# Two transformer blocks in one fp32 kernel: the first block's inverse roots multiplied into the accumulators, GpSimd's low parts in pieces, and two smaller moves

## The chip, the cores and the metric

One core of one Trainium2 chip. The metric is the device time of one execution in microseconds (us). PE is TensorE, ACT ScalarE, DVE VectorE, POOL GpSimd, SP SyncE, which issues most DMAs.

## What is computed

A residual stream x of 512 tokens by 1024 runs through two blocks of two layers each, all in float32. Block 1, in each layer:

```python
h = rms_norm(x, attn_norm_g[l])                 # x * rsqrt(mean(x*x) + eps) * g
rq, rk, rv, rg, dq, dk, dv = split(h @ w_in[l])
ret = rms_norm(retention_bidir(rq, rk, rv, ...), ret_norm_g[l]) * silu(rg)
da = rms_norm(diff_attention(norm(dq), norm(dk), dv, lam, slopes), diff_norm_g[l]) * (1 - lam_init)
x = x + concat([ret, da]) @ w_out[l]
h = rms_norm(x, ffn_norm_g[l])
x = x + (silu(h @ w_gate[l]) * (h @ w_up[l])) @ w_down[l]
```

Block 2 carries 256 context tokens beside the 512 in its first layer (768 columns), has neighbourhood attention in layer 0 and sliding-window attention (swa) in layer 1, a gated FFN with a depthwise convolution, and a modulation: `mod = silu(c) @ w_mod + b_mod` gives shifts, scales and gates, 96 rows of w_mod tiles in all, computed by DVE while block 1 runs.

## The kernel before

Everything is transposed: features on the 128 partitions, tokens (S = 512, or T2 = 768) along the free axis. xT holds the stream in 8 tiles. **A unit** is one 128-column slice of a weight matrix times all of h: K tiles (8, or 11 in the down projections), three matmuls each, since float32 is made from two fp32r parts (hi*hi + hi*lo + lo*hi). 364 units run in the order that schedule() lists. They go in pairs (par 0 and 1) over two sets of w_raw, w_hi and w_lo and two PSUM accumulators acc[0], acc[1].

The weights' chain of a unit: SP loads w_raw (weights, L500); once PE is done with the unit before the last, ACT casts it to w_hi (hi_part, L1178; each stage calls it as split(par) after mm_done); POOL writes w_lo = w_raw - w_hi in one instruction (L556); PE waits for w_lo_ready (unit, from L647). SP waits with the next w_raw until w_lo is ready. In the FFN's down projection the first pair interleaves its two units (LATE_LAST), since its last input tile comes late.

**Norms.** In the residual stage before a norm, DVE adds the accumulator to xT (L1808), ACT squares the tile (L1236), DVE sums six of the squares (L1815). PE packs the sums into one bank (L820), ACT takes the root (L1252), DVE inverts it (L1669), PE spreads it over the tokens (L827), and then, tile by tile: DVE multiplies x, gain and inverse root (n_xn, L1683), ACT makes h_hi (L1259), DVE or POOL h_lo (L1701, L612). The next pair of units (fresh_pair, L701) follows tile by tile. norm() runs so for all eight norms; at the start of the program it squares and packs each tile as it lands.

**After a unit.** In block 1's projections ACT copies the accumulator to proj1 (take_out, L1301; Silu for rg), and for dq, dk DVE does (head_norm, L1732), with a norm per head behind it: squares on ACT, sums (head_sums) and spreads (head_casts) on PE between the next units' matmuls, as `tail` for the last pair. In the gated FFN (glu, L1342 and L1825) unit par 0 is the gate, par 1 the up projection: ACT writes glu_g = Silu(acc[0]), DVE glu_a = acc[1] * glu_g (L1832), ACT b_hi, DVE b_lo (L1834). Silu, Sqrt and Exp need a table in ACT, loaded by an ACT_TABLE_LOAD where another one is in; Copy, in front of them in the first loop of an FFN, gets one too.

**Modulation** (L1626): per pair of units of block 1 two multiply-and-sum instructions on 128x1024 (L1634, L1637) and a copy of two columns (L1640), on DVE, from mod_w, which SP loads once the last pair's are done (mod_step). It stands in front of the takes in head_norm, resid and glu; beside projections DVE has nothing else.

ahead() moves the first pair's weights of a stage ahead of the norm or attention in front of it, on SP and POOL. In the swa stage SP waits for n_xn_ready (all of the norm) and loads cosine, sine and band before it loads q's weights.

## Time and profile before

| | us |
|---|---|
| median of 3 runs | 3073.2 (3066.57 to 3074.27) |
| the profiled execution | 3069.21 |
| its span, first to last instruction | 3067.4 |
| PE busy | 2981.4 (97%) |
| DVE busy | 1585.0 (52%) |
| ACT busy | 1144.6 (37%) |
| POOL busy | 1053.2 (34%) |

The mean granted clock of PE was 0.989 of full speed. A window row gives each engine's busy time in a stretch; a timeline row an instruction's start and length; behind an arrow stands what released it.

### The profile page before, as it was taken

To read this page: it belongs to the slowest core of one execution; us is meant where nothing else is said; L and a number is where in the kernel's file an instruction comes from. 1 tells how busy PE (TensorE), PEld (TensorE's weight loads), DVE (VectorE), ACT (ScalarE), POOL (GpSimd) and SP (SyncE) were. 2 spreads that over 40 slices of the span, in tenths; PEclk is the share of its full clock that TensorE was granted. 3 is DMA by queue.
4 is the path that set the end of the run, shared out by engine and by line. 5 is a ranking of instruction groups with operands and counts; after the bars stand their busy time and mean duration, and the time that the engine had idled before them with its cause. 6 is when DMAs were issued, how large, how long until landed. Compare 5 with 4: busy or idle time off the path is not lost.

```text
span 3067.4 us, 46468 instructions
## 1 busy us (share of the span) xinstructions
PE 2981.4 (97%) x16904; PEld 2398.4 (78%) x16904; DVE 1585.0 (52%) x2527; ACT 1144.6 (37%) x1735; POOL 1053.2 (34%) x458
## 2 busy tenths in 40 slices
PE   8999999999999999999999999999999899999999
PEld 6866788887857788877886687888888777878887
DVE  5357654556357544554315746541553348566372
ACT  4264441223274442232226733321332227543232
POOL 3433444443433444442220023332223240244443
PEclk9999999999999999999999999999999899999999
DMA  4421343433411344431111111121111110122222
GB/s 165 142 102 38 127 151 124 147 132 104 164 60 56 125 146 131 146 124 49 48 65 42 53 42 55 62 69 56 67 64 66 56 62 8 38 86 95 91 97 101
DMA packets 78029, 272.75 MB, mean 89 GB/s; under 512 B 8160, under 2 KB 15328, under 8 KB 77792
## 3 DMA queue, kind: packets, MB, share of 16 engines
q1 hardware_dynamic: 76256, 267.09, 26.2%
q10 hardware_dynamic: 1664, 4.18, 0.4%
q8 instruction: 72, 1.18, 0.2%
q14 instruction: 37, 0.30, 0.0%
HBM read 269.14 MB, written 2.10 MB: 88 GB/s over the span
## 4 chain that ended last, share of the span: by engine, by line
PE 58%; issue 26%; POOL 8%; DVE 5%; ACT 2%; POOLq 0%; DMA 0%; ACTq 0%; DVEq 0%
PE ps L663 43%; POOL w_lo L556 7%; PE ps L701 4%; PE ps L1085 1%; PE ps L772 1%; PE ps L1067 1%; PE ps L814 1%; DVE s_s L2081 1%; PE ps L928 1%; PE ps L917 1%; DVE s_s L2071 1%; PE ps L952 1%; PE ps L909 1%; DVE h_lo L1701 1%; PE ps L827 1%
## 5 line engine op out<-in xcount | busy, mean ns | idle before, releaser
L556 POOL TENSOR_TENSOR w_lo<-w_raw,w_hi 128x1024 fp32r<-128x1024 f32 (+1 forms) x364 | 945.0, 2596 | 1533.6 <-ACT w_hi L1178 1533.6
L663 PE MATMUL ps<-h_hi,w_hi 128*128 128x512 f32 (+1 forms) x2816 | 953.2, 372 | 8.2 <-POOL w_lo L556 4.2
L663 PE MATMUL ps<-h_hi,w_lo 128*128 128x512 f32 (+1 forms) x2816 | 945.1, 369 | 0.0
L663 PE MATMUL ps<-h_lo,w_hi 128*128 128x512 f32 (+1 forms) x2816 | 944.1, 368 | 0.0
L1178 ACT ACTIVATE w_hi<-w_raw 128x1024 fp32r<-128x1024 f32 (+1 forms) x364 | 406.4, 1116 | 1352.0 <-PE ps L663 1229.4
L663 PEld LDWEIGHTS ps<-h_hi,w_hi 128*128 128x128 f32 x2816 | 489.4, 188 | 116.2 <-issue 12.9
L663 PEld LDWEIGHTS ps<-h_hi,w_lo 128*128 128x128 f32 x2816 | 489.1, 188 | 90.8
L663 PEld LDWEIGHTS ps<-h_lo,w_hi 128*128 128x128 f32 x2816 | 488.4, 188 | 89.4 <-issue 0.7
L1855 DVE TENSOR_SCALAR conv_y<-u_pad,small 128x770 f32<-128x770 f32 (+1 forms) x88 | 176.3, 2004 | 192.2 <-ACT u_pad L1371 192.0
L1808 DVE SCALAR_TENSOR_TENSOR xT<-ps,mod,xT 128x512 f32 (+1 forms) x72 | 45.4, 659 | 306.7 <-PE ps L663 259.9
L1634 DVE CUSTOM_DVE_ANT_0 mod_junk<-mod_w,silu_c 128x1024 f32<-128x1024 f32 x96 | 139.3, 1451 | 123.5 <-DMA mod_w<-w_mod_dram 121.6
L1858 DVE SCALAR_TENSOR_TENSOR conv_y<-u_pad,small,conv_y 128x770 f32<-128x770 f32 (+1 forms) x176 | 156.1, 887 | 24.4 <-DVE conv_y L1855 6.7
L1637 DVE CUSTOM_DVE_ANT_0 mod_junk<-mod_w,silu_c 128x1024 f32<-128x1024 f32 x96 | 159.0, 1656 | 3.3
L1832 DVE TENSOR_TENSOR glu_a<-ps,glu_g 128x512 f32<-128x512 f32 x44 | 30.4, 692 | 188.7 <-PE ps L663 182.0
L1834 DVE TENSOR_TENSOR b_lo<-glu_a,b_hi 128x512 f32 x44 | 105.4, 2396 | 41.6 <-ACT b_hi L1352 41.6
L663 PE MATMUL ps<-a_hi,w_hi 128*128 128x512 f32 (+1 forms) x396 | 119.9, 357 | 1.5 <-POOL w_lo L556 1.5
L663 PE MATMUL ps<-a_lo,w_hi 128*128 128x512 f32 (+1 forms) x396 | 120.0, 357 | 0.0
L663 PE MATMUL ps<-a_hi,w_lo 128*128 128x512 f32 (+1 forms) x396 | 120.0, 357 | 0.0
L663 PE MATMUL ps<-b_hi,w_hi 128*128 128x512 f32 x264 | 104.8, 397 | 2.8 <-POOL w_lo L556 2.8
L663 PE MATMUL ps<-b_hi,w_lo 128*128 128x512 f32 x264 | 104.4, 396 | 0.0
L663 PE MATMUL ps<-b_lo,w_hi 128*128 128x512 f32 x264 | 104.4, 395 | 0.0
L1808 DVE SCALAR_TENSOR_TENSOR xT<-ps,xT 128x512 f32 (+1 forms) x48 | 33.2, 691 | 130.4 <-PE ps L663 104.4
(213 smaller groups left out, 3708.4 us busy)
## 6 DMA issues: line engine op xcount, KB each, us to landing
mod_w<-w_mod_dram SPq DMA_DIRECT2D x96, 512.0 KB, 3.5
w_raw<-w_gu_dram SPq DMA_DIRECT2D x88, 512.0 KB, 3.4
w_raw<-w_down_dram SPq DMA_DIRECT2D x64, 704.0 KB, 4.1
w_raw<-w_up_dram SPq DMA_DIRECT2D x88, 512.0 KB, 3.4
w_raw<-w_in_dram SPq DMA_DIRECT2D x56, 512.0 KB, 3.5
w_raw<-na_qkv_dram SPq DMA_DIRECT2D x24, 512.0 KB, 3.4
w_raw<-w_out_dram SPq DMA_DIRECT2D x16, 512.0 KB, 3.5
n_bias<-rpb_dram SPq DMA_DIRECT2D x24, 256.0 KB, 3.1
```

Source lines behind the costliest of these rows:

```text
L556: pool.tensor_tensor(w_lo[par][:, 0:cols], w_raw[par][:, 0:cols], w_hi[par][:, 0:cols].bitcast(F32), ALU.subtract).then_inc(w_lo_ready, 1)
L663: last = pe.matmul(acc[par][:, to:to + n], w[par][:, k * P:k * P + P], r[:, k, frm:frm + n], start=begin, stop=end)
L701: last = pe.matmul(acc[par][:, to:to + n], w[par][:, k * P:k * P + P], r[:, k, frm:frm + n], start=begin, stop=end)
L772: last[hd] = pe.matmul(bank(4 + 2 * (s % 2) + hd)[:, to:to + 2 * P], proj[half, j, queries], proj[half, 8 + j, keys], start=True, stop=True)
L814: pe.matmul(ps[:, 2048 + to:2048 + to + w], mats[half, SPREAD64 + g % 2, :], hn_rs[half, frm:frm + w], start=True, stop=True).then_inc(hn_ ...
L1178: act.activation(w_hi[par][:, 0:K * P], w_raw[par][:, 0:K * P], ACT.Copy).then_inc(w_hi_ready, 1)
L1634: dve.tensor_tensor_reduce(mod_junk[:], mod_w[:], silu_c[:, 0, :], 1.0, 0.0, ALU.mult, ALU.add, mod_sum[:, 0:1]).then_inc(mod_step, 1)
L1637: dve.tensor_tensor_reduce(mod_junk[:], mod_w[:], silu_c[:, 1, :], 1.0, 0.0, ALU.mult, ALU.add, mod_sum[:, 1:2]).then_inc(mod_step, 1)
L1808: last = dve.scalar_tensor_tensor(out=x_, in0=row(acc[par][:, to:to + n]), scalar=gate, in1=x_, op0=ALU.mult, op1=ALU.add)
L1834: dve.tensor_tensor(b_lo[:, bass.ds(f, 1), :], row(glu_a[:]), b_hi[:, bass.ds(f, 1), :].bitcast(F32), ALU.subtract).then_inc(a_lo_ready, 1)
L1855: dve.tensor_scalar(y, u, tap(0), tap(3), ALU.mult, ALU.add).then_inc(conv_step, 1)
L1858: dve.scalar_tensor_tensor(out=y, in0=u, scalar=tap(j), in1=y, op0=ALU.mult, op1=ALU.add).then_inc(conv_step, 1)
```

## The change

Seven edits, listed as what the code does:

1. Block 1's four norms become kind "late". ACT makes h_hi = xT * gain directly (hi_late), DVE h_lo from the same product; the inverse root, spread over the tokens, is kept in SBUF (rb) and multiplied in where the accumulators are taken. PE packs and spreads between the matmuls of the first pair, which runs unit 0 whole and then unit 1 (packs after step 3, spreads after step 10; at the start after 9 and 13). POOL does none of the low tiles.
2. So DVE, not ACT, takes block 1's projections (take_proj), with modulation between the two takes; rg's Silu then runs in place on ACT. In glu DVE writes glu_g = acc[0] * rb, then runs modulation, ACT takes Silu in place, DVE multiplies by rb again, then by acc[1].
3. At the start the gains are loaded first, by SP; w_raw is loaded without a wait for x's third part; the constants come last; ACT makes h_hi as x lands and squares afterwards.
4. POOL's w_lo is written by 4 instructions of a quarter each, its h_lo tiles by one per 256 columns.
5. The gated FFN's first round stands ahead of the loop in ACT's program (peel=1); a Silu on one element stands ahead of rg's.
6. In the swa stage SP loads q's first two pairs of weights before it waits for the norm and loads cosine, sine and band.
7. The casts of the swa keys' last pair come at step 10 of the next pair instead of 5.

```diff
-POOL_TILES = {"norm": (2, 4, 6), "mix": (0, 2, 5, 3, 6), "fin2": (0, 2, 4, 6)}
+POOL_TILES = {"late": (), "norm": (2, 4, 6), "mix": (0, 2, 5, 3, 6), "fin2": (0, 2, 4, 6)}
...
+        add("late" if block == 1 else "norm", block=block, layer=layer, which=which, T=T)
...
+                    weights(dict(ph, pairs=(0, 2)))
+                    sp.wait_ge(n_xn_ready, KT * (ph["norm0"] - 2 * DEPTH))
                     sp.dma_start(s_cos[:], d["rope"][0]).then_inc(tab["rope"], 16)
                     sp.dma_start(s_sin[:], d["rope"][1]).then_inc(tab["rope"], 16)
                     sp.dma_start(s_band[:], d["band"]).then_inc(tab["swa"], 16)
                 if "weight" in ph:
-                    weights(ph)
+                    weights(dict(ph, pairs=(2, 4)) if roped(ph) else ph)
...
-                        pool.tensor_tensor(w_lo[par][:, 0:cols], w_raw[par][:, 0:cols],
-                                           w_hi[par][:, 0:cols].bitcast(F32), ALU.subtract).then_inc(w_lo_ready, 1)
+                        for frm in range(0, cols, cols // PIECES):
+                            piece = slice(frm, frm + cols // PIECES)
+                            last = pool.tensor_tensor(w_lo[par][:, piece], w_raw[par][:, piece],
+                                                      w_hi[par][:, piece].bitcast(F32), ALU.subtract)
+                        last.then_inc(w_lo_ready, 1)
...
+                order = LATE_LAST if hidden else alternate(KT if late else 6 if ph["T"] == S else 3)
+                for step, (par, k) in enumerate(order):
...
+                    if late and step == (9 if first else 3):
+                        pack_norm(ph["fresh"])
+                    if late and step == (13 if first else 10):
+                        spread_norm(ph["fresh"])
...
-                    if k == 5:
+                    if k == (KT + 2 if ph["T"] == T2 and n == 2 else 5):
...
+            def hi_late(ph, k):
+
+                gain = col("g_" + ph["which"], KT * ph["layer"] + k)
+                act.activation(h_hi[:, k, 0:S], xT[:, k, 0:S], ACT.Copy, scale=gain).then_inc(h_hi_ready, 1)
+
+            def root(ph):
+                act.wait_ge(n_sum, ph["chunk0"] + len(chunks(ph["T"])))
+                act.activation(n_rs[:], n_packed, ACT.Sqrt, bias=eps1[:]).then_inc(n_std, 1)
+
+            def late_end(ph, split):
+
+                n0 = ph["norm0"]
+                hi_late(ph, 0)
+                act.wait_ge(acc_free, ph["unit0"])
+                act.wait_ge(n_added, (KT - 1) * (n0 + 1))
+                act.activation(n_sq[1][:, 0:S], xT[:, KT - 1, 0:S], ACT.Square).then_inc(n_sq_ready, 1)
+                hi_late(ph, 1)
+                hi_late(ph, 2)
+                split(1)
+                for k in range(3, KT):
+                    hi_late(ph, k)
+                root(ph)
...
+            def beginning(ph):
+
+                act.wait_ge(gains_in, 16)
+                for q in range(4):
+                    act.wait_ge(x_in[q], 16)
+                    hi_late(ph, 2 * q)
+                    hi_late(ph, 2 * q + 1)
+                    if q in (0, 2):
+                        hi_part(q // 2, 16, KT)
+                act.dma_start(lam_vec[:], d["lam"]).then_inc(loaded, 16)
+                act.dma_start(silu_c[:], d["c"]).then_inc(loaded, 16)
+                act.activation(stats[:, 20:21], eps1[:], ACT.Sqrt).then_inc(table_in, 1)
+                for k in range(KT):
+                    if k >= 2:
+                        act.wait_ge(n_added, k)
+                    act.activation(n_sq[k % 2][:, 0:S], xT[:, k, 0:S], ACT.Square).then_inc(n_sq_ready, 1)
+                root(ph)
...
+                        if ph["weight"] == "w_in":
+                            split(par)
+                            if ph["func"] == "silu":
+                                gate = dst[:, bass.ds(i * 2 + (ph["tile0"] + par), 1), 0:S]
+                                act.wait_ge(acc_free, i * 2 + (ph["unit0"] + par + 1))
+                                act.activation(gate, gate, ACT.Silu)
+                            continue
...
-                    act.activation(glu_g[:], acc[0][:, 0:S], ACT.Silu).then_inc(acc_free, 1)
+                    act.wait_ge(acc_free, f * 2 + (ph["unit0"] + 1))
+                    act.activation(glu_g[:], glu_g[:], ACT.Silu).then_inc(glu_silu, 1)
...
-                units_of(ph, body)
+                units_of(ph, body, peel=1)
...
+            def late(ph):
+
+                n0 = ph["norm0"]
+                if n0 == 0:
+                    dve.wait_ge(gains_in, 16)
+                    dve.memset(n_sum_sq[:, 0:S], 0.0).then_inc(n_added, 1)
+
+                def lo(k):
+                    dve.wait_ge(h_hi_ready, KT * ph["h0"] + k + 1)
+                    dve.scalar_tensor_tensor(out=h_lo[:, k, 0:S], in0=xT[:, k, 0:S],
+                                             scalar=col("g_" + ph["which"], KT * ph["layer"] + k),
+                                             in1=h_hi[:, k, 0:S].bitcast(F32), op0=ALU.mult, op1=ALU.subtract
+                                             ).then_inc(h_dve, 1)
+
+                def invert():
+                    dve.wait_ge(n_std, n0 + 1)
+                    dve.reciprocal(n_rs[:], n_rs[:]).then_inc(n_recip, 1)
+
+                for k in range(KT):
+                    lo(k)
+                    if k == 5 and n0:
+                        invert()
+                if n0 == 0:
+                    for k in range(KT - 2):
+                        dve.wait_ge(n_sq_ready, k + 1)
+                        dve.wait_ge(n_added, k + 1)
+                        dve.tensor_tensor(n_sum_sq[:, 0:S], n_sum_sq[:, 0:S], n_sq[k % 2][:, 0:S], ALU.add
+                                          ).then_inc(n_added, 1)
+                    invert()
+                dve.wait_ge(n_cast, ph["chunk0"] + len(chunks(S)))
+                dve.tensor_copy(halves(row(rb[:])), spread_out(S)).then_inc(n_rb, 1)
+
+            def inverted(ph):
+
+                dve.wait_ge(n_rb, ph["norm0"])
+
+            def take_proj(ph):
+
+                inverted(ph)
+
+                def take(i, par):
+                    dve.wait_ge(mm_done, i * 2 + (ph["unit0"] + par + 1))
+                    dve.tensor_tensor(proj1[:, bass.ds(i * 2 + (ph["tile0"] + par), 1), :], row(acc[par][:, 0:S]), row(rb[:]),
+                                      ALU.mult).then_inc(acc_free, 1)
+
+                with dve.Fori(0, ph["units"] // 2) as i:
+                    take(i, 0)
+                    modulation(i, ph["unit0"])
+                    take(i, 1)
...
+                inverted(ph)
                 with dve.Fori(0, FH) as f:
+                    dve.wait_ge(mm_done, f * 2 + (ph["unit0"] + 1))
+                    dve.wait_ge(a_lo_ready, BEGUN + f + n0)
+                    dve.tensor_tensor(glu_g[:], acc[0][:, 0:S], rb[:], ALU.mult).then_inc(acc_free, 1)
                     modulation(f, ph["unit0"])
-                    dve.wait_ge(acc_free, f * 2 + (ph["unit0"] + 1))
+                    dve.wait_ge(glu_silu, f + (n0 + 1))
+                    dve.tensor_tensor(glu_g[:], glu_g[:], rb[:], ALU.mult).then_inc(glu_scaled, 1)
                     dve.wait_ge(mm_done, f * 2 + (ph["unit0"] + 2))
-                    dve.wait_ge(a_lo_ready, BEGUN + f + n0)
+                    dve.wait_ge(glu_scaled, f + (n0 + 1))
                     dve.tensor_tensor(glu_a[:], acc[1][:, 0:S], glu_g[:], ALU.mult).then_inc(acc_free, 1)
```

## Rows read from the trace of the kernel before

**Rows 1.** The page, busy us (share of the span) and instructions of TensorE.
```profile
PE 2981.4 (97%) x16904; PEld 2398.4 (78%) x16904; DVE 1585.0 (52%) x2527; ACT 1144.6 (37%) x1735; POOL 1053.2 (34%) x458
```

**Rows 2.** Waits of PE: us in total, times, longest us.
```profile
PE ps L827 <- DVE n_rs L1669: 9.8, 8, 1.8
...
PE ps L663 <- POOL w_lo L556: 8.5, 9, 3.6
...
PE ps L701 <- ACT h_hi L1259: 6.5, 4, 1.6
```

**Rows 3.** Windows: stretch and its us, busy of each engine, PEclk, DMA share, GB/s.
```profile
322.70:343.10 20.40, 15.71 (x113) 11.14 (x112) 12.91 (x21) 11.44 (x16) 8.59 (x5) 0.92 0.21 70
697.30:718.00 20.70, 16.28 (x112) 12.08 (x113) 15.47 (x21) 8.35 (x13) 8.60 (x5) 0.84 0.16 51
1003.80:1024.40 20.60, 16.21 (x113) 11.87 (x112) 12.88 (x21) 11.40 (x16) 8.60 (x5) 0.83 0.21 73
17.00:35.20 18.20, 14.64 (x48) 10.41 (x48) 15.99 (x31) 10.10 (x13) 8.18 (x5) 1.00 0.31 103
2439.00:2461.80 22.80, 17.21 (x83) 12.32 (x82) 6.97 (x6) 5.85 (x7) 7.08 (x3) 0.85 0.17 56
```

**Rows 4.** Timeline, 322.5 to 328.9: start, us, engine, line, operation [idle before].
```profile
322.63 0.43 PE L820 MATMUL ps<-n_sum_sq,mats 128*32 128x64 f32 x16
...
327.92 1.29 ACT L1259 ACTIVATE h_hi<-n_xn 128x512 fp32r<-128x512 f32 x2 [2.60 <-DVE n_xn L1683]
...
328.69 0.76 PE L701 MATMUL ps<-h_hi,w_hi 128*128 128x512 f32 x1 [1.63 <-ACT h_hi L1259]
```

**Rows 5.** Timeline around two weight units, at 564 and at 465.
```profile
564.12 1.06 ACT L1178 ACTIVATE w_hi<-w_raw 128x1024 fp32r<-128x1024 f32 x1 [3.91 <-PE ps L663]
...
565.26 2.39 POOL L556 TENSOR_TENSOR w_lo<-w_raw,w_hi 128x1024 fp32r<-128x1024 f32 x1 [3.13 <-ACT w_hi L1178]
...
569.28 0.39 PE L663 MATMUL ps<-h_hi,w_hi 128*128 128x512 f32 x1
...
465.23 3.21 POOL L556 TENSOR_TENSOR w_lo<-w_raw,w_hi 128x1408 fp32r<-128x1408 f32 x1 [8.05 <-ACT w_hi L1178]
...
468.57 0.49 PE L663 MATMUL ps<-b_hi,w_hi 128*128 128x512 f32 x1 [0.72 <-POOL w_lo L556]
```

**Rows 6.** Timeline of DVE and POOL, at 469 and at 1776.
```profile
468.73 1.23 DVE L1634 CUSTOM_DVE_ANT_0 mod_junk<-mod_w,silu_c 128x1024 f32<-128x1024 f32 x1
...
469.34 3.69 POOL L556 TENSOR_TENSOR w_lo<-w_raw,w_hi 128x1408 fp32r<-128x1408 f32 x1 [0.91 <-ACT w_hi L1178]
...
469.99 4.12 DVE L1637 CUSTOM_DVE_ANT_0 mod_junk<-mod_w,silu_c 128x1024 f32<-128x1024 f32 x1
...
1776.16 0.96 DVE L1979 TENSOR_TENSOR h_lo<-proj,h_hi 128x768 fp32r<-128x768 f32 x1 [0.46 <-ACT h_hi L1471]
...
1776.95 4.39 POOL L612 TENSOR_TENSOR h_lo<-proj,h_hi 128x768 fp32r<-128x768 f32 x2 [74.76 <-ACT h_hi L1471]
...
1777.64 4.52 DVE L1979 TENSOR_TENSOR h_lo<-proj,h_hi 128x768 fp32r<-128x768 f32 x2 [0.51 <-ACT h_hi L1471]
```

**Rows 7.** Groups by line and form: count, busy us, mean ns, idle before.
```profile
L556 POOL TENSOR_TENSOR w_lo<-w_raw,w_hi 128x1024 fp32r<-128x1024 f32 x300 | 728.4, 2428 | 1218.1 <-ACT w_hi L1178 1218.1
...
L612 POOL TENSOR_TENSOR h_lo<-n_xn,h_hi 128x768 fp32r<-128x768 f32 x9 | 16.6, 1843 | 42.7 <-ACT h_hi L1259 42.7
...
L572 POOL TENSOR_TENSOR x_mask<-x_mask,r_mid 128x128 f32<-128x128 f32 x8 | 3.7, 457 | 7.5 <-ACT x_mask L1276 7.5
...
L1863 DVE TENSOR_TENSOR a_lo<-conv_z,a_hi 128x512 f32 x20 | 13.7, 686 | 0.0
...
L1178 ACT ACT_TABLE_LOAD x20 | 25.7, 1283 | 75.7 <-PE ps L663 71.8 <-PE ps L701 3.9
```

**Rows 8.** Timeline of POOL and DVE in the last conv FFN.
```profile
2744.47 2.39 POOL L556 TENSOR_TENSOR w_lo<-w_raw,w_hi 128x1024 fp32r<-128x1024 f32 x1 [2.96 <-ACT w_hi L1178]
...
2745.15 2.00 DVE L1855 TENSOR_SCALAR conv_y<-u_pad,small 128x512 f32<-128x512 f32 x1 [0.96 <-ACT u_pad L1371]
```

More of the change, by code:

```diff
@@ L124, in norm @@
     def norm(block, layer, which, T):
-        add("norm", block=block, layer=layer, which=which, T=T)
+        add("late" if block == 1 else "norm", block=block, layer=layer, which=which, T=T)
         count["norm"] += 1
@@ L186, in schedule @@
         after["fresh"] = ph if "weight" in after and ph["kind"] in POOL_TILES else None
-        ph["norm_T"] = after["T"] if after["kind"] == "norm" else None
+        ph["norm_T"] = after["T"] if after["kind"] in ("late", "norm") else None
     return phases
@@ L228 @@
 EARLY = 3
+PIECES = 4
 FRESH_ORDER = [0, 1, 2, 4, 5, 3, 6, 7]
@@ L611, in lo_tiles @@
                     pool.wait_ge(h_hi_ready, 8 * ph["h0"] + k + 1)
-                    pool.tensor_tensor(h_lo[:, k, 0:T], source(k), h_hi[:, k, 0:T].bitcast(F32), ALU.subtract
-                                       ).then_inc(h_pool, 1)
+                    for frm in range(0, T, 2 * P):
+                        last = pool.tensor_tensor(h_lo[:, k, frm:frm + 2 * P], source(k)[:, frm:frm + 2 * P],
+                                                  h_hi[:, k, frm:frm + 2 * P].bitcast(F32), ALU.subtract)
+                    last.then_inc(h_pool, 1)
             for ph in ahead(phases):
@@ L681, in fresh_pair @@
                 u0, K = ph["unit0"], ph["K"]
-                hidden = K == FH
+                hidden, late = K == FH, ph["fresh"] and ph["fresh"]["kind"] == "late"
                 hi, lo = (h_hi, h_lo) if not hidden else (b_hi, b_lo) if u0 < MOD_UNITS else (a_hi, a_lo)
                 segs = segments(ph["T"], CTX_AT if hidden else S)
-                for par, k in LATE_LAST if hidden else alternate(6 if ph["T"] == S else 3):
+                order = LATE_LAST if hidden else alternate(KT if late else 6 if ph["T"] == S else 3)
+                for step, (par, k) in enumerate(order):
                     if k == 0:
@@ L853, in normed_units @@
                     unit(ph, 0, 0, first, ends[0])
-                    unit(ph, 0, 1, first)
+                    unit(ph, 0, 1, first, ends[0])
                 def pair(i):
@@ L1148, in _ @@
                 if kind == "norm":
-                    norm(ph)
+                    pack_norm(ph)
+                    spread_norm(ph)
                 elif kind == "normed":
@@ L1226, in resid @@
                     act.wait_ge(table_in, n0 + 2)
+                late = T is not None and ph["unit0"] < MOD_UNITS and ph["unit0"] + KT < MOD_UNITS
                 def body(i, split):
@@ L1230, in body @@
                         act.wait_ge(mm_done, i * 2 + (ph["unit0"] + par + 1))
+                        if late and isinstance(i, int) and i * 2 + par == KT - 1:
+                            late_end(phases[phases.index(ph) + 1], split)
+                            continue
                         split(par)
@@ L1287, in body @@
                 def body(i, split):
+                    if ph["func"] == "silu" and i == 0:
+                        act.activation(stats[:, 23:24], eps1[:], ACT.Silu)
                     for par in range(2):
                         act.wait_ge(mm_done, i * 2 + (ph["unit0"] + par + 1))
-                        dst = proj1 if ph["T"] == S and ph["weight"] == "w_in" else proj
+                        dst = proj1 if ph["weight"] == "w_in" else proj
+                        if ph["weight"] == "w_in":
[4 more added lines that the diff above has]
+                                act.activation(gate, gate, ACT.Silu)
+                            continue
                         if ph["weight"] == "na_qkv" and i == 3 and par == 0:
@@ L1302, in body @@
                                        row(acc[par][:, 0:ph["T"]]),
-                                       ACT.Silu if ph["func"] == "silu" else ACT.Copy).then_inc(acc_free, 1)
+                                       ACT.Copy).then_inc(acc_free, 1)
                         if ph["weight"] == "swa_qkv" and par == 0:
@@ L1561, in _ @@
                     norm(ph)
-                    if ph["norm0"] == 0:
-                        condition()
+                elif kind == "late" and ph["norm0"] == 0:
+                    beginning(ph)
+                    condition()
                 elif kind == "normed":
@@ L1679, in normed @@
                     for to, _, w, c in segments(T):
-                        gain = col("g_" + ph["which"], KT * ph["layer"] + k) if ph["block"] == 1 else \
-                            gs[:, ph["layer"], w_i, k, c:c + 1]
+                        gain = gs[:, ph["layer"], w_i, k, c:c + 1]
                         if T == S:
@@ L1689, in normed @@
                                 in1=sums[0][:, to:to + w], op0=ALU.mult, op1=ALU.mult)
-                    if ph["block"] == 2 and k in POOL_TILES["norm"]:
+                    if k in POOL_TILES["norm"]:
                         last.then_inc(n_scaled, 1)
@@ L1763, in head_norm @@
                 take(0, 1)
+                if beside and h0 == 0:
+                    modulation(0, ph["unit0"])
                 if roped(ph):
@@ L2103, in _ @@
                     norm(ph)
+                elif kind == "late":
+                    late(ph)
                     if ph["norm0"] == 0:
@@ L2109, in _ @@
                         decays()
+                elif kind == "proj" and ph["weight"] == "w_in":
+                    take_proj(ph)
                 elif kind == "proj":
```

79 lines of the change are left out of this document (35 added, 44 removed).

## The prediction

> **What bounds the kernel now.** The page's busy table comes first: TensorE (PE) has a matmul running for 97% of the span [rows 1], so a gain can only come from its few idle stretches, and a loss from any new one. The waits of PE say where it idles: behind the reciprocal of the norm's root, behind the first high part of a normed tile, and behind POOL's low part of the weights [rows 2]. The windows show what a norm costs. From the last matmul of the residual stage to the first matmul after the next pair of units, PE is busy 15.7 of 20.4 us, 16.3 of 20.7 and 16.2 of 20.6, at a mean granted clock of 0.92, 0.84 and 0.83; at the start 14.6 of 18.2, around q's first weights 17.2 of 22.8 at 0.85 [rows 3]. The timeline of one norm shows the chain: packs from 322.63, the first high part at 327.92, the first matmul at 328.69, six us later [rows 4].
>
> Everywhere else PE is full, and what matters is how much room the weights' chain has: matmuls of a unit done, ACT casts the high part (split in ACT), POOL subtracts (L556), PE starts the unit after the next. In the second half of a gated FFN [rows 5] ACT's cast starts at 564.12, POOL at 565.26, and PE needs the result for 569.28. PE starts 0.13 us after POOL ends (465.23 + 3.21 = 468.44 against 468.57). So, **counted from the start of ACT's cast, POOL starts at 1.14 and must end by 5.03** (569.28 - 564.12 - 0.13). With 2.4 us of work it ends at 3.54: 1.5 to spare.
>
> **The shared resource.** POOL and DVE hold each other up when DVE reads two operands in SBUF. While L1634 runs (to 469.96), POOL is ready at 469.34 and takes 3.69 instead of 3.21, ending 3.07 after L1634; L1637, ready at 469.99, takes 4.12 instead of 1.23 and ends 1.08 after POOL [rows 6]. So one holds the resource for a whole instruction, and the waiter then needs 0.14 less than its own time. Who goes first when both queue is shown at 1776.95 [rows 6]: two POOL instructions back to back take 4.39, against 2 x 1.84 [rows 7], while two DVE ones wait. The surplus 0.71 is one DVE instruction (0.96 less overlaps) let in between them. **They alternate.** The Trainium skill (SBUF — State Buffer, "SBUF: two separate sides") calls this an exclusive lock for the whole instruction, not split because deep queues would have to be drained. Read as holding over queued instructions, it would give the first rival below, about 3056; the trace has one clean case against it.
>
> **The change, part by part.**
>
> (a) Three norms in front of S-wide units. The high part now comes straight from xT times the gain, with the root multiplied in when the accumulators are taken. From ACT's start T after the last residual matmul (322.8 in rows 4): high part 0 to 0.65, PE starts at 0.75 instead of 5.9. ACT then does the last square, two high parts (0.65 each, rows 4), the cast of 1.06, five high parts: the last at 6.9. DVE does all eight low parts (0.7 each) and, from 3.8 on, alternates with POOL's pieces; it inverts the root after the sixth, so the last low part ends near 9.4. PE finishes unit 0 at about T+9.65, then needs 8 tiles x 3 x 0.227 = 5.4 for unit 1 and about 1 for the spreads: T+16.1. For the FFN norm of layer 0 that is 338.9 against 343.1 in the trace: 4.2 gained; for that of layer 1, 4.4. At layer 1's attention norm DVE runs modulation(0) before the first take, 3 us, and PE waits about 1.2 for its accumulator: 3.3. **Sum -11.9.** Bounds: 0 in each if PE's clock falls as in rows 3; -15 if DVE and POOL never meet.
>
> (b) Start. The first matmul no longer stands behind squares, packs and root, but the second pair's weights still stand behind ACT's root, two table loads and Silu of c. I take -2.5 of the 3.6 idle us of rows 3; bounds +2 (those later on ACT) and -8.
>
> (c) q's weights are issued ahead of n_xn_ready, and the casts move to the second unit. PE idles 5.6 us in that window [rows 3], 3.6 of it the longest wait for POOL [rows 2], the rest behind the heads' roots; I let all of it go, and the slow clock with it: 0.15 x 17.2 busy us = 2.6. **-8.2**; bounds -4 (the wait for POOL alone) and -10.
>
> (d) Silu's table. In the first halves a table load of 1.28 stands ahead of the cast, 20 times [rows 7], and so POOL ends 1.28 later, still inside the 1.5 of room. Hidden: **0**. It gives the weights' chain 1.28 of room there, which (f) uses up.
>
> (e) Pieces. POOL takes 0.46 for 128 columns and 2.40 for 1024 [rows 7]: 2.17 ns a column, 0.18 fixed. A piece of 256 is 0.73, four are 2.9 (+0.5); of 352, 0.94, four 3.8. Alone this hides in the 1.5 spare, except at the six first pairs of an FFN's down projection, where PE waits for POOL now (0.9 of each in rows 2): +0.5 each, **+3**.
>
> (f) Pieces with DVE's new work. This is where I see the loss. In the gated FFN, DVE now takes the gate (0.7) just when ACT casts, and **modulation comes right behind it**, with a second scaling of glu_g after Silu. From the start of ACT's cast: gate taken 0.05 to 0.75; L1634's instruction to 1.98; POOL, ready at 1.14, ends piece 1 at 2.57 (0.59 as a waiter); L1637's, waiting, at 3.65; piece 2 at 4.24; the 2-column copy at once; piece 3 at 4.83; the scaling (0.69 [rows 7] less 0.14) at 5.38; piece 4 at 5.97. That is 0.94 after 5.03, and PE idles 0.94 in every round. Of 44 rounds, two stand behind a norm with room, four cast the down projection: 38 x 0.94 = **+35.7**. The four have longer pieces (0.80 as a waiter) and end at 6.81: 4 x 1.78 = **+7.1**. The second unit of a round meets only b_lo and has room.
> In the projections DVE takes the accumulator, then modulates; no scaling: piece 4 ends at 4.83 + 0.73 = 5.56, 0.53 late, in 16 pairs: **+8.5**. In the residual of w_out, the sum of squares and then the next pair's modulation meet POOL: by the same steps 0.84 late, six times: **+5**. The down projections have units of 33 matmuls, and end inside their room.
> In the last conv FFN (S wide) DVE's first tap and two further taps fall between the pieces. POOL starts at 2744.47, the tap is ready at 2745.15, just before piece 1 would end at 2745.20 [rows 8], and w_lo ends 0.04 late: **+1**; bounds 0 and +9 (0.4 in each of 22 pairs). All other DVE additions lie on an engine busy about half the time, and new semaphore waits stand at points already passed: 0.
>
> **Sum.** -11.9 - 2.5 - 8.2 + 3 + 35.7 + 7.1 + 8.5 + 5 + 1 = +37.7. The profiled execution took 3069.2 (span 3067.4); the median of the runs shown is 3073.2, 4 above it. So 3107 for an execution like the profiled one, **3110 for the median** (3110.9, rounded down for the rounds' small gain from the table).
>
> **The rivals.** *POOL keeps the resource through its four pieces.* Then piece 4 of a gated round ends at 1.98 - 0.14 + 2.9 = 4.8, inside 5.03; DVE waits, as today. Only the four down-projection casts (0.6 each) and +3 of (e) remain: -22.6 + 2.3 + 3 = -17.3, **3056** for the median, faster. For it: pieces carry no wait of their own, the two of 1776.95 did. Against it: DVE got in there although both of POOL's were queued. It decides wherever DVE's second modulation instruction is waiting at a piece's end. *The modulation's transfer lands late*, so that L1634 falls behind POOL: only the scaling meets it, the rounds keep 10.9, about **3062 to 3072**. Against: SP issues mod_w once the last modulation is done, a round ahead. *The table does not stay*: the cast starts 1.28 later in 20 rounds, +26: **3136**. Against: the second halves load none already. *The clock falls in the new norms or in the gated rounds*, which idle 8% of their time: +10 to +20, 3120 to 3130.
>
> **How the numbers follow.** Alternation as worked out 0.72, with 3090 to 3126 as its own range; lock kept 0.15; late transfer 0.05; table 0.04; clock 0.04. Differences within 0.3% (9 us) can't be told from none. Slower takes the first, table and clock, less a little for a stall half as large: 0.77; same 0.05; faster 0.18. With 3 in 20 around 3056, the range must reach there: 3052 to 3130.
>
> **What would show it.** Right: in a gated round PE starts about 11.8 after the last one, waits for w_lo about 0.9, POOL's four pieces spread over some 4.8 us with L1637's instruction near 1.7; PE's waits for w_lo rise from 8.5 to some 60; no table loads in the rounds; the three norm windows shrink by 3 to 4 and the swa start by 8. Wrong: rounds of 10.9 with four pieces in 2.9 us and L1637 at over 3, or pieces that alternate but end inside 5.03.

## The result: slower by 1.7%

The changed kernel takes 3124.4 us (median of 4 runs, 3119.2 to 3126.8) against 3070.3 for the kernel before beside it: ratio 1.017, 95% interval 1.015 to 1.020. The forecast was 3110 and slower, with a range of 3052 to 3130. The medians are 54.0 apart, where the forecast had some 37. The profiled execution has a span of 3124.8, 57.4 more than that of before.

The profile after. First the lines of the page that answer to [rows 1] and [rows 2] (busy us and instructions; the chain that ended last):

```profile
PE 2994.0 (96%) x16824; PEld 2384.0 (76%) x16824; DVE 1524.0 (49%) x2646; ACT 1079.7 (35%) x1668; POOL 1460.8 (47%) x1571
...
PE 45%; POOL 26%; issue 23%; DVE 4%; ACT 2%; POOLq 0%; DMA 0%; DVEq 0%; ACTq 0%
PE ps L679 32%; POOL w_lo L569 25%; PE ps L718 3%; PE ps L1103 1%; PE ps L793 1%; PE ps L1085 1%; DVE s_s L2201 1%; PE ps L946 1%; PE ps L935 1%; DVE s_s L2191 1%; PE ps L927 1%; PE ps L970 1%; PE ps L835 1%; PE ps L959 1%; DVE n_xn L1747 0%
```

POOL's busy time rose by 408 us [rows 1], in 1113 more instructions; by the prediction's 0.18 each their fixed parts are 200 of that; most of the rest, by estimate, passes waiting for DVE inside them. Its low part of the weights, L569 here, now holds a quarter of the chain that ended last. PE's waits in the changed kernel (us in total, times, longest):

```profile
PE ps L679 <- DVE glu_a L1952: 30.6, 37, 0.9
PE ps L679 <- POOL w_lo L569: 24.6, 32, 5.5
PE ps L718 <- POOL w_lo L569: 20.9, 7, 12.8
...
PE ps L848 <- DVE n_rs L1730: 4.6, 4, 1.2
PE ps L841 <- ACT n_sq L1300: 4.3, 4, 1.3
```

The norms' waits of [rows 2] halved; the waits for w_lo grew from 8.5 to 45.5 (24.6 and 20.9). The first line names DVE's glu_a, in 37 rounds, 0.8 in the mean and 0.9 at most. A round is the two units of one pair, gate and up. The timeline of one gated round shows why the line names glu_a (start, us):

```profile
368.77 1.06 ACT L1195 ACTIVATE w_hi<-w_raw 128x1024 fp32r<-128x1024 f32 x1 [5.11 <-PE ps L679]
...
368.77 0.69 DVE L1946 TENSOR_TENSOR glu_g<-ps,rb 128x512 f32<-128x512 f32 x1 [4.27 <-PE ps L679]
369.38 1.21 DVE L1697 CUSTOM_DVE_ANT_0 mod_junk<-mod_w,silu_c 128x1024 f32<-128x1024 f32 x1
...
370.64 1.64 DVE L1700 CUSTOM_DVE_ANT_0 mod_junk<-mod_w,silu_c 128x1024 f32<-128x1024 f32 x1
...
372.81 0.68 DVE L1949 TENSOR_TENSOR glu_g<-glu_g,rb 128x512 f32<-128x512 f32 x1
374.12 0.69 DVE L1952 TENSOR_TENSOR glu_a<-ps,glu_g 128x512 f32<-128x512 f32 x1 [0.63 <-PE ps L679]
...
369.91 4.87 POOL L569 TENSOR_TENSOR w_lo<-w_raw,w_hi 128x256 fp32r<-128x256 f32 x4 [3.43 <-ACT w_hi L1195]
...
374.91 0.49 PE L679 MATMUL ps<-h_hi,w_hi 128*128 128x512 f32 x1 [0.82 <-DVE glu_a L1952]
```

POOL's four pieces start at 369.91, 1.14 after ACT's cast, and end at 374.78, 6.01 after it (5.97 was forecast); PE starts 0.13 later. DVE's glu_a ends at 374.81, 0.03 after POOL, so the profile names it, although PE doesn't need that accumulator for this unit. That is a coincidence of two ends, and a rival to test. The next round starts at 386.91: 12.00 where before had 10.91.

The windows that answer to [rows 3], each from the last matmul of the stage before to the first of the next pair:

```profile
334.60:351.00 16.40, 15.11 (x114) 10.30 (x113) 10.75 (x15) 9.78 (x14) 7.02 (x8) 1.00 0.17 57
730.40:747.50 17.10, 15.28 (x113) 10.10 (x112) 11.73 (x18) 7.94 (x13) 7.01 (x8) 1.00 0.11 32
1043.90:1060.30 16.40, 15.10 (x114) 10.32 (x114) 10.78 (x15) 9.78 (x14) 7.00 (x8) 1.00 0.13 44
12.80:35.10 22.30, 15.55 (x113) 11.92 (x113) 14.30 (x31) 16.64 (x22) 8.59 (x9) 0.97 0.33 122
2498.40:2512.90 14.50, 14.50 (x81) 10.90 (x81) 6.97 (x6) 4.22 (x5) 5.61 (x8) 1.00 0.55 186
```

The norms went from 20.4, 20.7 and 20.6 to 16.4, 17.1 and 16.4, the stretch around q's weights from 22.8 to 14.5 with PE never idle, all four at the full granted clock. The parts meant to help did help. The start begins 4.2 earlier (12.84), and its second pair stands where it stood (35.06 against 35.25), with PE idle 6.8 of the 22.3 us between.

The 57.4 by stages, from the starts of PE's units in the two traces. "Casts of the down projection" are the last casts of each gated half: they already prepare the first weights of the down projection behind it, which have 1408 columns.

| stretch | forecast | measured |
|---|---|---|
| (a) three late norms | -11.9 | -12.3 |
| (b) start, until the projections | -2.5 | +1.0 |
| (c) q's first weights | -8.2 | -8.2 |
| (e) first pairs of the six down projections | +3 | +3.3 |
| (f) gated rounds, 38 | +35.7 | +42.2 |
| (f) casts of the down projection, 4 | +7.1 | +6.8 |
| (f) projections | +8.5 | +12.1 |
| (f) residual of w_out | +5 | +6.3 |
| last conv FFN and its neighbours | +1 | +3.9 |
| the rest (mix stages, the two-row stages) | 0 | +2.3 |

### The profile page after: what moved, and what is told of

Same layout as the page of the kernel before. It is cut to its first block, busy times and chain, and to the rows that moved or that the text cites. A ratio compares the mean times of both kernels' runs of the same rounds, so it can differ in the third digit from the quotient of the medians.

```text
span 3124.8 us, 47388 instructions
## 1 busy us (share of the span) xinstructions
PE 2994.0 (96%) x16824; PEld 2384.0 (76%) x16824; DVE 1524.0 (49%) x2646; ACT 1079.7 (35%) x1668; POOL 1460.8 (47%) x1571
## 4 chain that ended last, share of the span: by engine, by line
PE 45%; POOL 26%; issue 23%; DVE 4%; ACT 2%; POOLq 0%; DMA 0%; DVEq 0%; ACTq 0%
PE ps L679 32%; POOL w_lo L569 25%; PE ps L718 3%; PE ps L1103 1%; PE ps L793 1%; PE ps L1085 1%; DVE s_s L2201 1%; PE ps L946 1%; PE ps L935 1%; DVE s_s L2191 1%; PE ps L927 1%; PE ps L970 1%; PE ps L835 1%; PE ps L959 1%; DVE n_xn L1747 0%
## 5 line engine op out<-in xcount | busy, mean ns | idle before, releaser
L569 POOL TENSOR_TENSOR w_lo<-w_raw,w_hi 128x256 fp32r<-128x256 f32 (+1 forms) x1456 | 1361.9, 967 | 1213.2 <-ACT w_hi L1195 1213.2
L679 PE MATMUL ps<-h_hi,w_hi 128*128 128x512 f32 (+1 forms) x2816 | 960.6, 374 | 52.1 <-DVE glu_a L1952 30.6
L1978 DVE SCALAR_TENSOR_TENSOR conv_y<-u_pad,small,conv_y 128x770 f32<-128x770 f32 (+1 forms) x176 | 203.9, 1158 | 24.4 <-DVE conv_y L1975 6.7
L1975 DVE TENSOR_SCALAR conv_y<-u_pad,small 128x770 f32<-128x770 f32 (+1 forms) x88 | 80.3, 912 | 239.1 <-ACT u_pad L1432 239.1
L1700 DVE CUSTOM_DVE_ANT_0 mod_junk<-mod_w,silu_c 128x1024 f32<-128x1024 f32 x96 | 158.5, 1651 | 3.3
L1697 DVE CUSTOM_DVE_ANT_0 mod_junk<-mod_w,silu_c 128x1024 f32<-128x1024 f32 x96 | 126.2, 1315 | 6.3 <-DMA mod_w<-w_mod_dram 5.8
L627 POOL TENSOR_TENSOR h_lo<-proj,h_hi 128x256 fp32r<-128x256 f32 x20 | 16.6, 860 | 240.4 <-ACT h_hi L1532 240.4
L1946 DVE TENSOR_TENSOR glu_g<-ps,rb 128x512 f32<-128x512 f32 x44 | 30.4, 691 | 174.0 <-PE ps L679 173.4
```

Source lines behind the costliest of these rows:

```text
L569: last = pool.tensor_tensor(w_lo[par][:, piece], w_raw[par][:, piece], w_hi[par][:, piece].bitcast(F32), ALU.subtract)
L679: last = pe.matmul(acc[par][:, to:to + n], w[par][:, k * P:k * P + P], r[:, k, frm:frm + n], start=begin, stop=end)
L1697: dve.tensor_tensor_reduce(mod_junk[:], mod_w[:], silu_c[:, 0, :], 1.0, 0.0, ALU.mult, ALU.add, mod_sum[:, 0:1]).then_inc(mod_step, 1)
L1700: dve.tensor_tensor_reduce(mod_junk[:], mod_w[:], silu_c[:, 1, :], 1.0, 0.0, ALU.mult, ALU.add, mod_sum[:, 1:2]).then_inc(mod_step, 1)
L1975: dve.tensor_scalar(y, u, tap(0), tap(3), ALU.mult, ALU.add).then_inc(conv_step, 1)
L1978: dve.scalar_tensor_tensor(out=y, in0=u, scalar=tap(j), in1=y, op0=ALU.mult, op1=ALU.add).then_inc(conv_step, 1)
```

## The experiments

My theory, A: POOL's pieces let DVE's waiting instructions in, one at each piece's end, so w_lo ends after PE needs it. B: DVE's own new work on the accumulators (take, scale) is what PE waits for, as the named wait for glu_a suggests. C: the pieces' fixed cost. Each ratio below is to the kernel before on the same chip, with its 95% interval.

**One piece, and two.** In the changed kernel:

```diff
-PIECES = 4
+PIECES = 1
```

> The changed kernel with POOL's low part of the weights in one instruction again (the late norms, the new start, Silu's table, the early weights of q, and the pieces of the normed tiles stay). Theory A (POOL's pieces let DVE's waiting instructions in): the gated rounds fall from 12.0 back to about 10.9 us, the projections' pairs from 11.5 to 10.9, the pairs of w_out from 12.0 to 11; PE's wait for w_lo falls from 46 us to under 12. Some 42 x 1.1 + 16 x 0.65 + 6 x 1.0 = 63 less: 3061 (3054 to 3067). Theory B (DVE's own new work, taking and scaling each accumulator, is what PE waits for): the rounds stay near 12 and the total near 3115 to 3124. Theory C (only the fixed cost of the pieces, 0.5 a unit): 3124 less about 20, 3100 to 3108.

> The changed kernel with two pieces instead of four. Theory A: counted from the start of ACT's cast, DVE's first reduction ends at 1.98, POOL's first half (512 columns, 1.15 as a waiter) at 3.13, DVE's second reduction at 4.21, the second half at 5.36, which is 0.33 late: gated rounds of about 11.3 to 11.4, projections 11.2 to 11.3, casts of the down projection 1.2 late. Some 30 above the run with one piece: 3090 (3080 to 3098). Theory B: no difference from four pieces, 3115 to 3124. Theory C (fixed cost only): a third of the difference between one piece and four.

One piece: 3066.2 us, ratio 0.998 (0.997 to 0.999), inside my range. Two: 3070.1, 0.9996 (0.999 to 1.001), a miss: 10 below the range of 3080 to 3098. The loss is gone with the pieces, which B does not allow, and C explains 0.5 of 1.1 in a round. With one piece the rounds are 10.88, and PE's waits no longer name glu_a:

```profile
PE ps L679 <- POOL w_lo L569: 7.6, 9, 1.6
```

```profile
363.91 2.92 POOL L569 TENSOR_TENSOR w_lo<-w_raw,w_hi 128x1024 fp32r<-128x1024 f32 x1 [3.14 <-ACT w_hi L1195]
...
364.61 3.29 DVE L1700 CUSTOM_DVE_ANT_0 mod_junk<-mod_w,silu_c 128x1024 f32<-128x1024 f32 x1
```

(The first fence is PE's waits, the second the timeline of one round, both of the run with one piece.) The second reduction now waits out POOL: 3.29 instead of 1.64, and nobody needs it. One piece won back 5 less than the middle of my expectation, two pieces cost 20 less. With two, the gated rounds are 0.32 longer (11.20, where I had written 11.3 to 11.4), w_out's eight units stay at 49.4, and the pairs behind the late norms keep most of what pieces give them: in layer 0's gated FFN the first pair and the gap behind it take 18.1 with one piece, 15.8 with two, 15.3 with four. There DVE's eight low parts stand on the path, and a whole w_lo of POOL in between holds them up. **Pieces help in three places**, the first pairs behind the three late norms inside the kernel, **and harm in some seventy.** At the start they help nothing: PE's first matmul stands at 12.84 with four pieces and at 11.10 with one.

**The modulation shortened.** The changed kernel, four pieces, its reductions in the gated rounds over 16 columns, so that this kernel leaves the other 1008 columns out of those sums; taking and scaling the gate are unchanged.

```diff
-                    modulation(f, ph["unit0"])
+                    modulation(f, ph["unit0"], 16)
```

> The changed kernel with four pieces, in whose gated rounds alone the two reductions of the modulation run over 16 columns instead of 1024 (so that part of the modulation is left out of the result). Theory A: only the scaling of the gate meets POOL, whose fourth piece ends at 4.5, 0.5 before PE needs it: gated rounds of 10.9 us instead of 12.0, projections still 11.5. Total 3124 less 42 x 1.1: 3078 (3070 to 3084). Theory B (taking and scaling the gate, both still there): rounds stay near 12, total over 3115.

3075.8 us, ratio 1.002 (1.001 to 1.003): 48 gone, rounds of 10.88, projections still 11.5. The two timelines, DVE and POOL in a round of this run:

```profile
369.20 0.84 DVE L1949 TENSOR_TENSOR glu_g<-glu_g,rb 128x512 f32<-128x512 f32 x1 [0.30 <-ACT glu_g L1409]
372.95 0.69 DVE L1952 TENSOR_TENSOR glu_a<-ps,glu_g 128x512 f32<-128x512 f32 x1 [2.91 <-PE ps L679]
...
368.73 3.30 POOL L569 TENSOR_TENSOR w_lo<-w_raw,w_hi 128x256 fp32r<-128x256 f32 x4 [2.25 <-ACT w_hi L1195]
```

The four pieces take 3.30 where they took 4.87: only the scaling came in. With no DVE instruction waiting they take 2.83, as the changed kernel's own timeline shows for a round of the projections:

```profile
115.08 2.83 POOL L569 TENSOR_TENSOR w_lo<-w_raw,w_hi 128x256 fp32r<-128x256 f32 x4 [0.97 <-ACT w_hi L1195]
```

B falls: taking and scaling are still there, glu_a starts 5.35 after the same cast in both kernels (372.95 and 367.60 here, 374.12 and 368.77 there), and PE doesn't wait. The wait named after glu_a was one for w_lo.

**The kernel before, with pieces.** Nothing of the change but the four pieces, first in both units of a pair, then in the first unit alone.

```diff
-                        pool.tensor_tensor(w_lo[par][:, 0:cols], w_raw[par][:, 0:cols],
-                                           w_hi[par][:, 0:cols].bitcast(F32), ALU.subtract).then_inc(w_lo_ready, 1)
+                        for frm in range(0, cols, cols // 4):
+                            piece = slice(frm, frm + cols // 4)
+                            last = pool.tensor_tensor(w_lo[par][:, piece], w_raw[par][:, piece],
+                                                      w_hi[par][:, piece].bitcast(F32), ALU.subtract)
+                        last.then_inc(w_lo_ready, 1)
```

> The kernel before, with POOL's low part of the weights in four pieces and nothing else changed. Theory A: in the second half of a gated round the low part b_lo and both reductions of the modulation come between the pieces; by the same steps the fourth ends at 6.36 against 5.03: 1.3 late, rounds of 12.2 to 12.4 us instead of 10.9, so some 44 x 1.4 = 60 in the gated FFNs and a few more elsewhere: 3135 (3115 to 3150), slower than before by as much as the change itself. Theory C (fixed cost only, hidden in 1.5 us of room): 3070 to 3077. Theory B (new work of DVE needed for the loss): also 3070 to 3077.

> The kernel before with four pieces only for each pair's first unit, beside which DVE has no reduction; the second unit's low part stays whole. Theory A (pieces cost little where DVE does not queue): the second halves stay at 10.88, the first halves, whose table load leaves 0.34, get 0.3 longer in 20 rounds, the first pairs of the down projections 0.4: 3078 (3072 to 3083), against 3144 with pieces in both units. Theory C (splitting costs by itself): half of what e4_before_pieces lost, 3105.

In both units: 3144.4, ratio 1.024 (1.022 to 1.026), worse than the whole change. Rounds of 12.31, and the pieces now end late in the second unit, where the kernel before has b_lo and the modulation. In the first unit alone: 3086.0, 1.004 (1.003 to 1.006): second halves 10.88, first halves 11.24 (0.33 more), as the steps said. The total is a miss, 3 above my range and 8 above its middle. Some 4 of that is the last block, which I had left out: there each gap between the conv rounds and the down projection went from 0.22 to 1.32, with 0.6 more in each first pair. The rest isn't shown to belong to the pieces: the profiled execution has 4.5 more than before around the swa projections and attention, and e11_before_peel, with the code of before there, has 3.2 more. Splitting costs little by itself, and a neighbour in DVE's queue makes it dear.

**The modulation behind the scaling.** The changed kernel, four pieces, the same instructions in another order.

```diff
-                    modulation(f, ph["unit0"])
                     dve.wait_ge(glu_silu, f + (n0 + 1))
                     dve.tensor_tensor(glu_g[:], glu_g[:], rb[:], ALU.mult).then_inc(glu_scaled, 1)
+                    modulation(f, ph["unit0"])
```

> The changed kernel, four pieces, with both reductions of the modulation behind the second scaling of the gate in the gated rounds instead of ahead of it; the work is the same. Theory A (strict alternation at the pieces' ends): now the scaling (0.55) and both reductions (1.08 each) come between the pieces, the fourth ends at 6.36 against 5.03, 1.33 late instead of 0.94: gated rounds of 12.2 to 12.4, the casts of the down projection 2.1 late: 3135 (3130 to 3142). Theory B (the gate's path through Silu and scaling sets the loss): the scaling comes 2 us earlier, so rounds of 11.5 or less, total under 3110.

3149.8, ratio 1.026 (1.024 to 1.028). The second halves have rounds of 12.36, inside the 12.2 to 12.4 of the steps; scaling the gate earlier did not help, as B would have it. The total is a miss, 15 above the middle of my expectation and 8 above its range. The order has a second victim, seen at the second round of the first half, 14.31 long, and again at the third, 13.98. Timeline of this run, ACT and then SP's queue:

```profile
356.81 1.06 ACT L1195 ACTIVATE w_hi<-w_raw 128x1024 fp32r<-128x1024 f32 x1 [3.85 <-DMA w_raw<-w_gu_dram]
...
351.29 0.33 SPq L517 DMA_DIRECT2D mod_w<-w_mod_dram  x1
352.34 2.05 SPq L508 DMA_DIRECT2D w_raw<-w_gu_dram  x2
```

SP issues the next mod_w only when both reductions are done, and the raw weights stand behind it in the same queue. ACT's cast at 356.81 had waited 3.85 for them.

**Each small part alone**, in the kernel before: q's weights and the later casts of the heads; and the first round of a gated half outside ACT's loop.

```diff
                 if roped(ph):
+                    weights(dict(ph, pairs=(0, 2)))
                     sp.wait_ge(n_xn_ready, KT * ph["norm0"])
...
-                    weights(ph)
+                    weights(dict(ph, pairs=(2, 4)) if roped(ph) else ph)
...
-                    unit(ph, 0, 1, first)
+                    unit(ph, 0, 1, first, ends[0])
...
-                    if k == 5:
+                    if k == (KT + 2 if ph["T"] == T2 and n == 2 else 5):
```

```diff
-                units_of(ph, body)
+                units_of(ph, body, peel=1)
```

> The kernel before with one part of the change alone: q's first two pairs of weights issued ahead of the wait for the normed tiles, and the heads' casts of the context pair moved from tile 5 of the first unit to tile 2 of the second. Theory A: the window from the last matmul of the context pair to the first of q's second pair falls from 22.8 to 14.6 us, 8.2 less: 3063 (3059 to 3067). Rival (what the earlier weights give is lost again in the stage behind it): 3068 to 3072.

> The kernel before with one line changed: ACT's loop over a gated half runs its first round outside the loop, so that no table is loaded inside it (40 loads of 1.28 gone if the step is right). The prediction's step: the load stood inside the room of the weights' chain, so POOL's work in the first halves starts 1.28 earlier and PE gains nothing: rounds 10.88 instead of 10.90, total 3070 (3066 to 3073). Rival (the loads held PE up): 20 to 40 less.

q's weights: 3059.7, ratio 0.997 (0.996 to 0.998), 9.5 less; from the first matmul of the swa keys to that of the values behind q, 87.6 became 79.5. The loop: 3071.1, ratio 1.000 (0.999 to 1.001). The 40 table loads are gone, the first halves' rounds are 10.88 instead of 10.91, and no time is gained: the loads were hidden.

**A better version.** The changed kernel with four pieces only in the second unit behind each late norm (the start among them).

```diff
-PIECES = 4
+PIECES = {}
...
+    PIECES.update({(p["unit0"], 1): 4 for p in phases if p.get("fresh") and p["fresh"]["kind"] == "late"})
...
                     for par in range(2):
+                        n = PIECES.get((u0, par), 1) if isinstance(i, int) and i == 0 else 1
```

> The changed kernel with four pieces only in the second unit of the three stages behind a late norm (among them the start); every other low part of the weights in one instruction. Theory A: pieces are needed where DVE's eight low parts of the fresh tiles stand beside POOL, and harmful elsewhere. From the run with one piece everywhere the first pair behind each late norm loses its 2.7 to 3 us more (18.1 back to 15.3 in layer 0's gated FFN), the start some 2: 3066 less 10, 3056 (3052 to 3061), faster than the kernel before by 15. Theory D (those pairs were late for another reason, such as the clock): 3063 to 3068.

3055.6 us, ratio 0.996 (0.995 to 0.998): **14 faster than the kernel before and 69 faster than the change**. (The second figure is against the 3124.4 above; by the two ratios it is some 65.) The pair behind the norm of layer 0 takes 15.3 again. What is left are three of the four casts of the down projection (gap 1.29 instead of 0.23; the fourth has 0.23) and a raw weight that comes late at Silu's projections (2 us); that it comes late because SP waits for the longer reductions was not tested.

I then tried to take the casts' 1.06 away by moving the modulation, in two ways.

```diff
-                    modulation(f, ph["unit0"])
                     dve.wait_ge(glu_silu, f + (n0 + 1))
                     dve.tensor_tensor(glu_g[:], glu_g[:], rb[:], ALU.mult).then_inc(glu_scaled, 1)
+                    reduction(f, ph["unit0"], 0)
...
                                       b_hi[:, bass.ds(f, 1), :].bitcast(F32), ALU.subtract).then_inc(a_lo_ready, 1)
+                    reduction(f, ph["unit0"], 1)
+                    keep(f, ph["unit0"])
```

> The kernel of the run e5_late_only, with the two reductions of the modulation placed differently in the gated rounds: the first behind the second scaling of the gate, the second behind b_lo. Theory A: POOL then always starts before DVE wants the shared resource, so the stall of 1.06 at each of the four casts of the down projection goes as well: 4 less, 3052 (3048 to 3058), rounds of 10.9. Theory E (the second reduction lets the next modulation weights land too late, or the scaling behind POOL makes glu_a late): rounds over 11.2, total over 3070.

3313.3, ratio 1.079 (1.078 to 1.081): a miss, and rival E's; rounds take 16 to 18 us. A window and timelines of this run, within one round (the last two lines are SP's queue):

```profile
424.00:433.90 9.90, 7.20 (x21) 5.76 (x22) 8.18 (x7) 2.23 (x4) 5.12 (x2) 0.66 0.00 0
```

```profile
432.56 1.22 DVE L1701 CUSTOM_DVE_ANT_0 mod_junk<-mod_w,silu_c 128x1024 f32<-128x1024 f32 x1
...
433.97 0.33 SPq L518 DMA_DIRECT2D mod_w<-w_mod_dram  x1
434.95 1.03 SPq L509 DMA_DIRECT2D w_raw<-w_gu_dram  x2
```

For ten microseconds the window shows no byte moved: SP stands before mod_w until the second reduction is done at the round's end, and the raw weights of the next units behind it. PE idles, and the granted clock falls to half for part of the stretch (0.66 in the mean). The second way has the modulation at the top of the round from the second round on:

```diff
+                def body(f):
+                    if not isinstance(f, int):
+                        modulation(f, ph["unit0"])
```

> The kernel of the run e5_late_only, with the modulation of the gated rounds at the top of the round from the second round on, behind the previous b_lo and ahead of taking the gate, where the kernel before has it; SP's next weights then wait for reductions that end about 1.1 into the round (in e6_late_reordered they waited for one that ends at the round's end, and PE waited for the weights). Theory A: POOL starts each low part before DVE wants the shared resource, and the 1.06 at each cast of the down projection goes: the gap between the gated rounds and the down projection 0.23 instead of 1.29, four times, 4 less: 3051 (3048 to 3056). Rival F (the late take of the gate pushes Silu, the scaling and glu_a back until a round is longer): rounds over 11.1, total over 3062.

> The changed kernel itself, on the same chip beside the run above: 3124 (3118 to 3130), and a second profile of it, to see which stretches repeat. Theory: the gated rounds (12.0), the projections (11.5), the casts of the down projection (1.93) and the last stages (1.31) come out the same to 0.05; the 1.7 more in the mix stages, the 2 to 4 more in the first stage behind a two-row norm and the 1 more around the heads of the last block do not repeat, as they stand where the granted clock fell. Rival: they repeat, and belong to the change.

3057.4, ratio 0.995 (0.994 to 0.997): the four gaps are 0.22 to 0.24 as theory A said, the rounds 10.88, but the total lies 1 above my range and isn't told apart from e5_late_only's. In the profiled executions the start, up to the projections, took 3.3 longer than that run's with the same code there, as much as the three casts gave back (3 x 1.06).

The changed kernel again: 3120.6, ratio 1.017 (1.015 to 1.018). The gated rounds, projections, casts (1.93) and the last block (1.31) repeat to 0.05 each. The 1.7 in the first mix stage doesn't, nor does the 1.7 in the second. Windows in the first, of the first profile and then of this one:

```profile
204.00:212.00 8.00, 6.26 (x24) 2.39 (x24) 4.89 (x15) 5.07 (x12) 0.46 (x1) 0.79 0.00 0
```

```profile
204.00:212.00 8.00, 6.27 (x35) 3.04 (x34) 6.17 (x19) 5.80 (x14) 0.45 (x1) 1.00 0.00 0
```

The same busy time, 24 matmuls against 35, at a granted clock of 0.79 against 1.00. The stage behind the first two-row FFN's norm did repeat (191.9 twice), against my theory. With w_lo whole it takes 190.7, so about 1.2 belongs to the pieces. The other 3.4 of its difference to the profiled before (187.3) don't belong to the change: e7_before_q and e11_before_peel, whose code there is that of before, also take 190.7. Their ten rounds behind the first take 16.96 us each, those of the profiled before 16.64, all at a granted clock of 1.00; e2_two, with two pieces, has 16.64 again. What sets these two lengths is open.

## Why the prediction was right

The sign and the cause were right: POOL and DVE alternate at the pieces' ends. The Trainium skill's page "SBUF — State Buffer", section "SBUF: two separate sides", has the port held by one of the two for a whole instruction; the trace agrees for one instruction (3.29 for a reduction behind a whole w_lo). It doesn't extend to queued instructions: the rival *POOL keeps the resource through its four pieces* fell with the first round (4.87 for four pieces that take 2.83 at 115.08, where DVE asks for nothing). The transfer of the modulation was not late, the table stayed (no load in the rounds), the clock did not fall in the norms. PE's waits for w_lo, which I put at some 60, are 45.5 under that name and 30.6 more under glu_a's.

The size was less right than the sign: 54.0 between the medians where I had 37, and 3124.4 lies near the upper end of my own range for alternation (3090 to 3126).

By its terms. **(a)** and **(c)** came out to 0.4. **(d)** nothing, as its own run shows. **(e)** right in place and size. **(f)**, the loss, was undersized: its four rows sum to 67.4 where I had 56.3, and that is 11 of the 20 us between the forecast's sum (37.7) and the two spans (57.4). Each round lost 1.11 instead of 0.94. The wait itself was right: POOL ended 6.01 after the cast, PE started 0.98 past the point that the step named. But PE's unit then also runs longer, a term that the sum put at nothing: it takes 5.56 to 5.59 when it starts out of a wait, 5.44 when it follows without one, in every one of these rounds. Of the 0.13, 0.10 lies between its first two matmuls (0.33 apart instead of 0.23); why is not shown. The same 0.13 is missing from the projections (POOL's end 5.52 after the cast, 5.56 forecast; loss 0.65 instead of 0.53) and from w_out. There are also 18 stalled projection pairs, not 16. The four casts of the down projection came out at 1.71 against 1.78. The other 9 of the 20 us are (b), 3.5, the last block, 2.9, and the stages that I put at 0, 2.3. In (e) I had read 0.9 of waiting per first pair; the trace has 0.7, which enters no sum.

**(b)** failed by size: I took 2.5, and the trace has +1.0. The reason that the step named, the second pair's high part behind ACT's root and tables (29.15), is there, and POOL's pieces beside the first take and modulation then take 4.74 instead of 2.36. With that part whole, in three runs with equal code at the start, the second pair starts at 32.64, 34.25 and 34.38 instead of 35.06. So the stage's own scatter is as large as what there is to explain: from PE's first matmul to the projections it took 62.8 and 66.0 in the first and the last of these, and the unchanged start ended, with the projections' first matmul, at 75.85, 76.54 and 77.24. So (b) is zero within some 2 us, and it was not tested alone.

**The last block** was priced at 1. The steady rounds have room, as the step said, but I had looked only at casts of 1024 columns. The cast of 1408 beside the taps ends late too, by 1.1, at two places (1.31 against 0.22), and the kernel before with pieces in the first units has the same 1.32. These two are 2.2 of the 3.9; 0.8 more is the first pair behind the norm (16.17 against 15.39, and 15.55 with w_lo whole). The 0.7 in the stage in front of it is its first unit; it is there with w_lo whole too, so it isn't w_lo's pieces, and its cause is open.

## What to carry to other kernels

Before splitting a POOL instruction so that DVE needn't wait, look at who waits for which: each piece's end lets one queued DVE instruction with two operands in SBUF in, so split only where DVE's work is on the path, and keep POOL whole where its result is. A stall costs more than the wait, here 0.13 us of slower start each time. And before moving an instruction, follow the semaphore that a DMA queue waits on: what stands behind that DMA moves with it.

## What the runs showed of the hardware

- POOL and DVE alternate instruction by instruction when both queue, where DVE's reads two operands in SBUF. With one of them in PSUM it isn't held: glu_a takes its own 0.69 beside POOL's last piece at 374.12. The granularity sets who loses: with four pieces of 256 columns a round loses 1.1, with two of 512 0.3, with one nothing; with four pieces and the same instructions of DVE in another order it loses 1.5.
- A matmul unit (24 matmuls of 512 columns) takes 5.44 us when it follows the last, 5.56 to 5.59 when it starts out of a wait.
- The half granted clock isn't tied to the kernel: two profiles of the same kernel have it in different stretches, 1.7 us at a time, and two starts with equal code differ by 3.3. Ten rounds of 768 columns took 3.2 more in some executions than in others at the full granted clock, again with equal code. Differences of this size in one profile prove nothing.
